# Cutting the second product of U's blocks into 24 and 232 columns, in 73 of 128 blocks

## The chip, the cores and the metric

The kernel runs on one core of a Trainium2 chip. The metric is the device time of one execution in microseconds (us). Before the change the median of 3 runs is 1714.33 us (1714.15 to 1714.38).

## The reference

The reference is two transformer blocks in a row on 256 tokens of 1024 features. The first has two kinds of attention and, at its end, a product-key layer of 128 x 128 = 16384 single-neuron experts. That layer is where the change is:

```python
def per_chunk(args):
    xc, ec, gc = args
    u = expert_u[ec]
    a = jnp.einsum('cd,chkd->chk', xc, u).astype(jnp.float32)
    w = (jax.nn.gelu(a) * gc).astype(xc.dtype)
    return jnp.einsum('chk,chkd->cd', w, expert_v[ec])
```

`expert_u` and `expert_v` are 16384 x 1024. The second block has self attention, cross attention and a gated feed-forward layer, the last with 5632 columns in its first product, in each of two layers.

## The kernel before

**The experts are not gathered.** The kernel multiplies all tokens by all of `expert_u`, 128 rows of experts at a time (a block of U: 1024 features by 128 experts, for 256 tokens), takes the gelu, weighs it by a dense table of gates that is zero for the experts not chosen, and multiplies by all of `expert_v`.

**Three products for one.** A float32 product is made of three. Each operand stands in SBUF as a high part and a rest (`wsplit[..., 0, ...]` and `wsplit[..., 1, ...]` for the weights, `HT[:, 0]` and `HT[:, 1]` for the normed input). `mm3` issues high x high, high x rest and rest x high into one PSUM area. A block of U has 8 tiles of 128 features (`k` from 0 to 7), so 24 products, each a weight load of 128x128 and a matmul that streams 256 columns of `HT`. "The second product" of the title is the tile k = 1, with its three matmuls.

**U has two stretches.** The first 16 blocks (`EARLY`, line 1463 on) write the ring of four PSUM banks and come before the table of gates can be begun. Six transposes follow (L1475), and then the other 112 blocks (`BULK`, `times_u` at L1478 on, loop at L1513). In front of 64 of these blocks, evenly from m = 2 on, `gate_products` issues four matmuls of 256 columns on one-hot matrices (`hot_a`, `hot_b`), which make the table of gates for four tokens. `hot_groups_at(m)` says whether a group stands before block m; there is never more than one.

**The order** is written out by hand, engine by engine. For U, ScalarE makes the high part of a block (L1967) when the block three places before has been multiplied, GpSimd makes the rest (L1657; VectorE for 14 of the early ones), and TensorE waits for that by `u_made(n)` and, from m = 2, for the gelu that empties its PSUM bank.

**A cut already stands elsewhere.** The first products of the feed-forward layers (`ffu`) go through `feature_tile`, which, for six of the first column tiles of each layer (`DIVIDED`), issues k = 1 by `mm3_divided`: the high x high matmul is cut into columns 0 to 23 and 24 to 255, so four matmuls and four weight loads in place of three. There the input `HT` also begins 16 float32 (64 bytes) further on in its tensor:

```python
DIVIDED = {"ffu": {(0, 1): 24, (1, 0): 24, (1, 1): 24, (2, 0): 24, (2, 1): 24, (3, 0): 24}}
HT_BEGINS = {"ffn0": 16, "ffn1": 16}
```

For U, `HT` is `HT_at("norm1")`, which begins at 0. In the built program HT lies at byte 22016 of a partition and wsplit at 38912, both multiples of 512; in the feed-forward layers the input therefore begins 64 bytes past such a multiple.

Of the kernel before, what the change touches and what calls it, by code (L numbers as in the profile page):

```python
# [15 lines left out]
S = 256  # L16
# [188 lines left out]
def block_stack(nc: bass.Bass, x, mem, weights, expert_u, expert_v, small, layer1, band, wide_gains, out):  # L205
    with ExitStack() as ctx:
# [20 lines left out]
        PS = [ctx.enter_context(nc.psum_tensor(f"bank{b}", [P, 512], F32))[:, :] for b in range(4)]  # L227
# [3 lines left out]
        def HT_at(name):  # L231

            at = HT_BEGINS.get(name, 0)
            return HT_room[:, at:at + 2 * KD * S].rearrange("p (b k s) -> p b k s", b=2, k=KD)

        HT = HT_at("norm1")
# [37 lines left out]
        c = Columns()  # L274
# [7 lines left out]
        c = Columns()  # L282
# [47 lines left out]
        c = Columns()  # L330
# [34 lines left out]
        def hot_block(g):  # L365

            return FIRST_HOT + g * HOT_SPAN // HOT_GROUPS

        def hot_groups_at(m):

            return [g for g in range(HOT_GROUPS) if hot_block(g) == m]
# [13 lines left out]
        def u_slot(n):  # L385

            return n % 3 + 1
# [9 lines left out]
        def u_made(n):  # L397

            if n in U_BY_VECTOR:
                return u_lo_v, n - U_BY_VECTOR.start + 1  # L400
            return u_lo, n + 1 - (len(U_BY_VECTOR) if n >= U_BY_VECTOR.stop else 0)
# [36 lines left out]
        c = Columns()  # L438
# [431 lines left out]
        def _(pe):  # L870
            state = {"frees": 0}

            def mm(out, lhsT, rhs, start, stop, **kw):

                ins = pe.matmul(out, lhsT, rhs, start=start, stop=stop, **kw)  # L875
                if state["frees"]:
                    ins.then_inc(w_freed, 1)
                    state["frees"] = 0
                return ins

            def mm3(out, left, right, start, stop, **kw):


                for n, (a, b) in enumerate(((0, 0), (0, 1), (1, 0))):
                    ins = mm(out, left(a), right(b), start and n == 0, stop and n == 2, **kw)
                return ins

            def mm3_divided(out, left, right, n):

                cols = out.shape[-1]  # L890
                for c in (slice(0, n), slice(n, cols)):
                    mm(out[:, c], left(0), right(0)[:, c], False, False, skip_group_check=True)
                mm(out, left(0), right(1), False, False, skip_group_check=True)
                return mm(out, left(1), right(0), False, False, skip_group_check=True)

            def weights_of(*name):

                u = UNIT[name]
                pe.wait_ge(*lo_made(u))
                state["frees"] = u not in (0, FIRST2)  # L900
                return lambda part: wsplit[:, u % NSPLIT, part, :]

            def tiles_of(w, **sizes):

                return lambda part: w(part).rearrange("p (k n) -> p k n", **sizes)

            def open_bank(name):

                q = GROUP[name]
                if q >= RING:  # L910
                    wait_freed(pe, GROUPS[q - RING][0])
                return PS[4 + q % RING]
# [279 lines left out]
            def first_branch(f):  # L1192

                b = open_bank(("up", f))
                w = tiles_of(weights_of("up", f), k=8)
                up_products(b, w, 0)
                return b, w
# [171 lines left out]
            for kv, at in enumerate((KC, VC)):  # L1369

                b = open_bank(("win2", kv))
# [11 lines left out]
            for kv in range(2):  # L1383

                b = open_bank(("hid", kv))
                for q in range(4):
                    w = tiles_of(weights_of("cmp", kv, q), k=4)
                    for kk in range(4):
                        k = 4 * q + kk
# [5 lines left out]
            for kv in range(2):  # L1395
                b = open_bank(("hidT", kv))
# [6 lines left out]
            for kv in range(2):  # L1403
                b = open_bank(("c2", kv))
# [13 lines left out]
            for f in range(KD):  # L1418
                if f < len(begun):
                    b, w = begun[f]  # L1420
                    state["frees"] = f > 0
                else:
                    b, w = first_branch(f)
# [14 lines left out]
            for m in range(8):  # L1438
# [11 lines left out]
                elif hp < 3:  # L1450
                    b = open_bank(("sc", m))
# [11 lines left out]
            for n in range(EARLY):  # L1463
                b = open_bank(("ua", n))
                pe.wait_ge(*u_made(n))
                w = tiles_of(lambda part: wsplit[:, u_slot(n), part, :], k=KD)
                for k in range(KD):
                    ins = mm3(b[:, 0:S], lambda a: w(a)[:, k, :], lambda c: HT[:, c, k, :], k == 0, k == KD - 1)
                ins.then_inc(bank_full, 1)
            pe.wait_ge(ex_done, 1)  # L1470
            for m in range(3):
                b = open_bank(("et", m))
# [5 lines left out]
            def times_u(m):  # L1478

                pe.wait_ge(*u_made(m + EARLY))  # L1480
                if m >= 2:
                    pe.wait_ge(a_gelu, m - 1)
                w = tiles_of(lambda part: wsplit[:, u_slot(m + EARLY), part, :], k=KD)
                for k in range(KD):
                    ins = mm3(PS[m % 2][:, 0:S], lambda a: w(a)[:, k, :], lambda c: HT[:, c, k, :], k == 0, k == KD - 1)
                ins.then_inc(a_full, 1)

# [25 lines left out]
            for m in range(BULK):  # L1513
                for g in hot_groups_at(m):
                    if g == 0:
                        for n in range(3):
                            wait_freed(pe, ("et", n))
                    gate_products(g)
                times_u(m)
# [30 lines left out]
            for m in range(5):  # L1550
                if m == 4:
                    values_of_memory(1, [0])
                b = open_bank(("qkt2", m))
# [11 lines left out]
            for i in range(DEPTH2):  # L1565
                if i:
# [4 lines left out]
                    for g in range(4):  # L1571
                        if g == 2:
                            mem_key(2, 1)
                        b = open_bank(("pm", g))
# [15 lines left out]
                    for g2 in range(2):  # L1590
                        w = weights_of("pool", g2)
# [74 lines left out]
        def _(act):  # L1666
# [110 lines left out]

            def attention(use, split_behind):
                _, _, Pb, Tb = USES[use]
                j0 = JOBS[use]  # L1780

# [356 lines left out]
        def _(dve):  # L2138
# [241 lines left out]

            def attention(use, last_queries):
                jobs, _, Pb, _ = USES[use]
                j0 = JOBS[use]

# [665 lines left out]
```

## Time and profile before

| | us |
|---|---|
| median of 3 runs | 1714.33 |
| the profiled execution | 1714.29 |
| its span in the trace | 1712.5 |
| TensorE busy | 1699.6 (99%) |
| VectorE, ScalarE, GpSimd busy | 1236.9, 919.6, 383.0 |
| all waits of TensorE that the profile lists, in the whole span | 6.2 |

The span is what the trace covers; 1.8 us of the execution lie around it. PE is TensorE's matmul, PEld its weight load. A row of the timeline joins neighbouring instructions of one kind: its first number is the start of the first, its second the time from there to the end of the last, so (second number - duration of one) / (count - 1) is the distance from start to start. A row joins matmuls of different widths when they have the same operands, and then names the width of the first. A matmul's duration (some 280 ns) is longer than the distance to the next, since matmuls overlap.

### The profile page before, as it was taken

Reading aid. Unit: us, or ns where it says so; the run is one execution under the profiler, and the core shown is the slowest. Engines: PE = TensorE matmul, PEld = TensorE weight load, DVE = VectorE, ACT = ScalarE, POOL = GpSimd, SP = SyncE. Lnnn points to the kernel's source line nnn. Section 1 sums busy time; section 2 is a strip of 40 time slices with the busy share of each in tenths; the row PEclk is TensorE's granted clock in tenths of the full one; section 3 lists DMA queues with packets and bytes.
Section 4 is the critical chain, followed back from the end, with each engine's and each line's share of the span. In section 5 each row is a group of like instructions: output and inputs, shape, how many; then the busy total and the mean of one; then the engine's idle time right before and its main releaser. Section 6 shows DMA issues by size and latency. Waiting matters only on the chain.

```text
span 1712.5 us, 31053 instructions
## 1 busy us (share of the span) xinstructions
PE 1699.6 (99%) x11336; PEld 1544.7 (90%) x11336; DVE 1236.9 (72%) x2436; ACT 919.6 (54%) x1449; POOL 383.0 (22%) x172
## 2 busy tenths in 40 slices
PE   9999999999999999999999999999999999999998
PEld 8897999899999999988888888877899988889997
DVE  6748749875555555488888887876789966769974
ACT  6568654554545555533333334576476645566653
POOL 1130077437777777500000000000000000000000
PEclk9999999999999999999999999999999999999999
DMA  8561665577777777777777797635545564445562
GB/s 307 197 238 36 193 197 171 199 218 211 206 210 207 212 205 211 226 246 242 238 241 243 266 328 235 231 131 172 198 167 196 197 204 149 164 147 184 190 208 72
DMA packets 120453, 346.54 MB, mean 202 GB/s; under 512 B 13328, under 2 KB 45200, under 8 KB 118928
## 3 DMA queue, kind: packets, MB, share of 16 engines
q1 hardware_dynamic: 118480, 336.70, 61.5%
q10 hardware_dynamic: 1856, 8.23, 1.3%
q8 instruction: 79, 1.29, 0.3%
q14 instruction: 38, 0.31, 0.1%
HBM read 321.03 MB, written 23.86 MB: 201 GB/s over the span
## 4 chain that ended last, share of the span: by engine, by line
PE 95%; ACT 2%; DVE 1%; issue 0%; DMA 0%; POOL 0%; ACTq 0%; DVEq 0%
PE banks L875 60%; PE bank L875 33%; PE bank L1279 1%; ACT wsplit L1680 0%; DVE wsplit L2147 0%; ACT probs L1832 0%; ACT H L1714 0%; PE banks L1279 0%; DMA X<-x 0%; PE bank L930 0%; ACT H L1720 0%; PE bank L1141 0%; PE banks L1092 0%; POOL wsplit L1657 0%; PE bank L942 0%
## 5 line engine op out<-in xcount | busy, mean ns | idle before, releaser
L875 PE MATMUL banks<-HT,wsplit 128*128 128x256 f32 (+1 forms) x3532 | 432.1, 284 | 1.3 <-POOL wsplit L1657 0.6
L875 PEld LDWEIGHTS banks<-HT,wsplit 128*128 128x128 f32 x3532 | 421.0, 189 | 10.3 <-issue 3.4
L1967 ACT ACTIVATE wsplit<-raw 128x1024 fp32r<-128x1024 f32 x252 | 266.4, 1058 | 212.2 <-PE banks L875 201.2
L875 PE MATMUL banks<-wsplit,wexp 128*128 128x512 f32 x1536 | 348.3, 389 | 0.0
L875 PEld LDWEIGHTS banks<-wsplit,wexp 128*128 128x128 f32 x1536 | 288.3, 188 | 59.7
L875 PE MATMUL bank<-HT,wsplit 128*128 128x256 f32 x2688 | 333.2, 283 | 0.0
L875 PEld LDWEIGHTS bank<-HT,wsplit 128*128 128x128 f32 x2688 | 327.2, 192 | 0.0
L1657 POOL TENSOR_TENSOR wsplit<-raw,wsplit 128x1024 fp32r<-128x1024 f32 x114 | 275.4, 2416 | 131.1 <-ACT wsplit L1967 131.1
L1680 ACT ACTIVATE wsplit<-raw 128x1024 fp32r<-128x1024 f32 x146 | 154.3, 1059 | 96.7 <-PE bank L875 48.1
L2147 DVE TENSOR_TENSOR wsplit<-raw,wsplit 128x1024 fp32r<-128x1024 f32 x124 | 151.6, 1235 | 67.3 <-ACT wsplit L1680 66.1
L2730 DVE TENSOR_TENSOR wsplit<-raw,wsplit 128x1024 fp32r<-128x1024 f32 x128 | 156.1, 1219 | 6.2 <-ACT wsplit L1967 6.2
L2751 DVE TENSOR_TENSOR gates<-banks,gates 128x512 f32<-128x512 f32 x64 | 44.3, 692 | 148.3 <-ACT gates L2031 148.3
L2147 DVE TENSOR_TENSOR wsplit<-raw1b,wsplit 128x1024 fp32r<-128x1024 f32 x101 | 121.4, 1220 | 41.1 <-ACT wsplit L1680 40.7
L1680 ACT ACTIVATE wsplit<-raw1b 128x1024 fp32r<-128x1024 f32 x102 | 107.6, 1059 | 73.8 <-PE bank L875 41.9
L875 PE MATMUL bank<-wsplit,ff 128*128 128x512 f32 x528 | 120.1, 389 | 0.0
L875 PEld LDWEIGHTS bank<-wsplit,ff 128*128 128x128 f32 x528 | 98.9, 188 | 20.6
L875 PE MATMUL banks<-wsplit,HT 128*128 128x512 f32 (+1 forms) x432 | 93.6, 378 | 0.0
L875 PEld LDWEIGHTS banks<-wsplit,HT 128*128 128x128 f32 x432 | 78.2, 188 | 14.9
L2870 DVE SCALAR_TENSOR_TENSOR cv<-banks,smalls,cv 128x255 f32<-128x255 f32 x176 | 76.9, 478 | 11.2 <-ACT cv L2119 8.4
L1629 POOL TENSOR_TENSOR wsplit<-raw,wsplit 128x1024 fp32r<-128x1024 f32 x20 | 48.0, 2402 | 164.9 <-ACT wsplit L1680 164.9
L2766 DVE CAST wexp<-act_e 128x256 fp32r<-128x256 f32 x126 | 37.1, 294 | 61.5 <-PE banks L875 61.4
L1661 POOL TENSOR_TENSOR wsplit<-raw1b,wsplit 128x1024 fp32r<-128x1024 f32 x1 | 2.4, 2409 | 349.5 <-DVE wsplit L2147 349.5
(333 smaller groups left out, 2022.6 us busy)
## 6 DMA issues: line engine op xcount, KB each, us to landing
raw<-weights SPq DMA_DIRECT2D x148, 512.0 KB, 4.0
raw<-expert_v SPq DMA_DIRECT2D x128, 512.0 KB, 3.6
raw<-expert_u SPq DMA_DIRECT2D x124, 512.0 KB, 3.9
raw1b<-weights SPq DMA_DIRECT2D x102, 512.0 KB, 4.2
raw1a<-weights SPq DMA_DIRECT2D x48, 512.0 KB, 4.5
HT<-acts_parked SPq DMA_DIRECT2D x124, 128.0 KB, 3.4
acts_parked<-act_e SPq DMA_DIRECT2D x62, 128.0 KB, 3.9
acts_parked<-ropeg SPq DMA_DIRECT2D x62, 128.0 KB, 3.8
```

Source lines behind the costliest of these rows:

```text
L875: ins = pe.matmul(out, lhsT, rhs, start=start, stop=stop, **kw)
L1279: ins = pe.transpose(turned_bank(use, j)[:, at:at + P], Pb[:, j % 4, t, kt * P:(kt + 1) * P], ident)
L1629: pool.tensor_tensor(wsplit[:, s % NSPLIT, 1, :], sb_raw(n0 + s), f32(wsplit[:, s % NSPLIT, 0, :]), ALU.subtract).then_inc(lo_made(n0 + s) ...
L1657: pool.tensor_tensor(wsplit[:, u_slot(n), 1, :], u_raw(n), f32(wsplit[:, u_slot(n), 0, :]), ALU.subtract).then_inc(u_lo, 1)
L1661: pool.tensor_tensor(wsplit[:, (FIRST2 + 1) % NSPLIT, 1, :], sb_raw(FIRST2 + 1), f32(wsplit[:, (FIRST2 + 1) % NSPLIT, 0, :]), ALU.subtract ...
L1680: act.activation(wsplit[:, u % NSPLIT, 0, :], sb_raw(u), ACT.Copy).then_inc(w_hi, 1)
L1967: act.activation(wsplit[:, s, 0, :], src, ACT.Copy).then_inc(e_hi, 1)
L2147: dve.tensor_tensor(wsplit[:, u % NSPLIT, 1, :], sb_raw(u), f32(wsplit[:, u % NSPLIT, 0, :]), ALU.subtract).then_inc(lo_made(u)[0], 1)
L2730: dve.tensor_tensor(wsplit[:, s, 1, :], raw0[:, s, :], f32(wsplit[:, s, 0, :]), ALU.subtract).then_inc(v_lo, 1)
L2751: dve.tensor_tensor(gates_of(g), hot_half(g, 0), gates_of(g), ALU.add).then_inc(hot_out, 1)
L2766: dve.tensor_copy(wexp[:, s % 2, 0, :], w).then_inc(a_hi, 1)
L2870: ins = dve.scalar_tensor_tensor(out=y, in0=u[:, v], scalar=w, in1=y, op0=ALU.mult, op1=ALU.add)
```

## The change

In the first six early blocks and in bulk blocks 0 to 5 and all in front of which one-hot products stand, tile k = 1 goes through `mm3_divided` with 24 columns. `mm3_divided` itself stands in the kernel before.

```diff
@@ early blocks
                 for k in range(KD):
+                    if n < 6 and k == 1:
+                        mm3_divided(b[:, 0:S], lambda a: w(a)[:, k, :], lambda c: HT[:, c, k, :], 24)
+                        continue
                     ins = mm3(b[:, 0:S], lambda a: w(a)[:, k, :], lambda c: HT[:, c, k, :], k == 0, k == KD - 1)
@@ times_u(m)
                 for k in range(KD):
+                    if (m < 6 or hot_groups_at(m)) and k == 1:
+                        mm3_divided(PS[m % 2][:, 0:S], lambda a: w(a)[:, k, :], lambda c: HT[:, c, k, :], 24)
+                        continue
                     ins = mm3(PS[m % 2][:, 0:S], lambda a: w(a)[:, k, :], lambda c: HT[:, c, k, :], k == 0, k == KD - 1)
```

That is 6 early blocks, and 64 + 3 = 67 bulk blocks (0, 1 and 4 have no one-hot products in front): 73 cuts, 73 more matmuls and weight loads. TensorE at the first early blocks, in the program before (`memN` is the turning of the memory that ends just before U):

```order
L978 MATMUL bank<-smalls,memN 128x128 x16
L875 MATMUL banks_7<-HT,wsplit 128x256 x24
L875 MATMUL banks_5<-HT,wsplit 128x256 x48
L875 MATMUL banks_7<-HT,wsplit 128x256 x48
```

and in the changed one:

```order
L978 MATMUL bank<-smalls,memN 128x128 x16
L875 MATMUL banks_7<-HT,wsplit 128x256 x3
L875 MATMUL banks_7<-HT,wsplit 128x24
L875 MATMUL banks_7<-HT,wsplit 128x232
L875 MATMUL banks_7<-HT,wsplit 128x256 x20
L875 MATMUL banks_5<-HT,wsplit 128x256 x3
L875 MATMUL banks_5<-HT,wsplit 128x24
```

Nothing is moved: one matmul of 256 columns has become two, at the fourth place of a block. In the bulk, TensorE around a group of one-hot products (`hot_a`), before:

```order
L875 MATMUL bank<-HT,wsplit 128x256 x48
L875 MATMUL banks_5<-wsplit,hot_a 128x256 x4
L875 MATMUL bank<-HT,wsplit 128x256 x48
L875 MATMUL banks_7<-wsplit,hot_a 128x256 x4
L875 MATMUL bank<-HT,wsplit 128x256 x24
```

and now:

```order
L875 MATMUL bank<-HT,wsplit 128x256 x44
L875 MATMUL banks_5<-wsplit,hot_a 128x256 x4
L875 MATMUL bank<-HT,wsplit 128x256 x3
L875 MATMUL bank<-HT,wsplit 128x24
L875 MATMUL bank<-HT,wsplit 128x232
L875 MATMUL bank<-HT,wsplit 128x256 x44
L875 MATMUL banks_7<-wsplit,hot_a 128x256 x4
```

After the cut, 20 products of its own block follow and, where no group stands before the next block, 24 of that. The other four engines have the same instructions in the same order.

## Rows read from the trace of the kernel before

**Rows 1.** The page, busy time and the chain that ended last.

```profile
PE 1699.6 (99%) x11336; PEld 1544.7 (90%) x11336; DVE 1236.9 (72%) x2436; ACT 919.6 (54%) x1449; POOL 383.0 (22%) x172
...
PE 95%; ACT 2%; DVE 1%; issue 0%; DMA 0%; POOL 0%; ACTq 0%; DVEq 0%
```

**Rows 2.** TensorE's waits from 321 to 721 us: total, times, longest.

```profile
PE banks L875 <- POOL wsplit L1657: 0.6, 1, 0.6
```

**Rows 3.** Stretches: U's bulk, V, feed-forward 0; busy time, clock, DMA.

```profile
core 0: us, PE busy (x) PEld busy (x) DVE busy (x) ACT busy (x) POOL busy (x), PEclk, DMA share, GB/s
367.70:721.10 353.40, 353.40 (x2947) 353.40 (x2946) 197.71 (x265) 180.98 (x291) 265.84 (x111) 1.00 0.73 209
721.10:1069.60 348.50, 348.37 (x1538) 288.24 (x1537) 279.83 (x510) 138.99 (x133) 2.41 (x1) 1.00 0.79 256
1254.30:1374.80 120.50, 120.50 (x1064) 120.50 (x1063) 110.74 (x191) 74.25 (x109) 0.00 (x0) 1.00 0.56 192
```

**Rows 4.** Timeline of TensorE in U's bulk: start, time, instructions.

```profile
500.32 0.64 PE L875 MATMUL banks<-wsplit,hot_a 128*128 128x256 f32 x4
500.80 5.92 PE L875 MATMUL bank<-HT,wsplit 128*128 128x256 f32 x48
506.56 0.64 PE L875 MATMUL banks<-wsplit,hot_a 128*128 128x256 f32 x4
```

**Rows 5.** Timeline of feed-forward 0 after its sixth cut.

```profile
1272.14 102.84 PE L875 MATMUL banks<-HT,wsplit 128*128 128x256 f32 x906
1374.82 0.39 PE L875 MATMUL bank<-wsplit,ff 128*128 128x512 f32 x1
```

**Rows 6.** Groups by shape: matmuls (PE) and weight loads (PEld), feed-forward 0, then U.

```profile
L875 PE MATMUL banks<-HT,wsplit 128*128 128x256 f32 x797 | 90.5, 276 | 0.0
...
L875 PE MATMUL bank<-HT,wsplit 128*128 128x256 f32 x2429 | 301.4, 283 | 0.0
...
L875 PEld LDWEIGHTS banks<-HT,wsplit 128*128 128x128 f32 x796 | 90.3, 188 | 0.0
...
L875 PEld LDWEIGHTS bank<-HT,wsplit 128*128 128x128 f32 x2428 | 295.8, 192 | 0.0
```

**Rows 7.** Timeline of feed-forward 0 up to its first cut and through it.

```profile
1254.34 3.23 PE L875 MATMUL banks<-HT,wsplit 128*128 128x256 f32 x26
...
1257.52 14.78 PE L875 MATMUL banks<-HT,wsplit 128*128 128x24 f32 x129
...
1257.55 1.16 PE L875 MATMUL banks<-HT,wsplit 128*128 128x232 f32 x8
...
1257.74 0.96 PE L875 MATMUL banks<-HT,wsplit 128*128 128x256 f32 x7
...
1257.86 0.84 PE L875 MATMUL banks<-HT,wsplit 128*128 128x256 f32 x6
...
1257.97 2.76 PE L875 MATMUL banks<-HT,wsplit 128*128 128x256 f32 x23
```

**Rows 8.** Timeline at the sixth cut of feed-forward 0.

```profile
1271.68 0.73 PE L875 MATMUL banks<-HT,wsplit 128*128 128x24 f32 x5
```

**Rows 9.** Timeline at the start of U's bulk, one start per row.

```profile
367.74 0.27 PE L1475 MATMUL banks<-smalls,pick 128*128 128x128 f32 x1
367.76 0.60 PE L875 MATMUL bank<-HT,wsplit 128*128 128x256 f32 x3
...
367.97 0.52 PE L875 MATMUL bank<-HT,wsplit 128*128 128x256 f32 x3
...
368.08 0.52 PE L875 MATMUL bank<-HT,wsplit 128*128 128x256 f32 x3
...
368.20 5.56 PE L875 MATMUL bank<-HT,wsplit 128*128 128x256 f32 x45
```

**Rows 10.** Timeline of the early blocks, after the wait of 0.6 us.

```profile
327.24 39.88 PE L875 MATMUL banks<-HT,wsplit 128*128 128x256 f32 x331
```

**Rows 11.** GpSimd's rests of U in 374 to 721 us; durations in ns.

```profile
L1657 POOL TENSOR_TENSOR wsplit<-raw,wsplit x109: 2396/2413/2417, 372.4 to 714.1; 128x1024 fp32r<-128x1024 f32 x109
its engine sat idle before it (us, times) until:
  ACT wsplit L1967: 82.5, 109
```

## The prediction

> **What bounds the kernel.** I read the page first: TensorE is busy for 99% of the span and holds 95% of the chain that ended last [rows 1]. Its waits come next: in all of U it waits once, for 0.6 us, before the bulk [rows 2]. The stretches say the same and give the clock: 353.4 us busy of 353.4 in the bulk at the full 2.4 GHz (granted clock 1.00) [rows 3]. So U lasts as long as the distance from one matmul's start to the next, times their number, and the question is what the cut does to that distance. A matmul more adds to the end; a shorter distance takes off it.
>
> **Two paces for the same instruction.** In the bulk, 48 products take 5.92 us with the last one's 0.28: 5.64 / 47 = 120.0 ns from start to start, and the one-hot groups keep it (500.32 to 500.80 is four times 120) [rows 4]. In the feed-forward layer, after its cuts, 906 products of the same shape run at (102.84 - 0.28) / 905 = 113.3 ns [rows 5]. The durations show the difference too: 276 against 283 ns for the matmul, 188 against 192 for the weight load [rows 6]. Before the first cut that stretch runs at neither: 1254.34 to 1257.52 for 27 products is 117.8 ns [rows 7]. So the feed-forward layer differs from U in two ways, the cut and the input that begins 64 bytes further on; without any cut it was already at 117.8 and not at 120.0, and the cut took it from there to 113.3. The trace has no cut over an input at 0 bytes. That is the unknown.
>
> **The price of a cut.** The four matmuls of a cut product start at 1257.52, 1257.55, 1257.74 and 1257.86, and the next one at 1257.97 [rows 7]: 0.34 us for the first three, then one ordinary distance of 0.11. From the first cut to the sixth there are 5 x 25 matmuls in 1271.68 - 1257.52 = 14.16 us, 113.3 ns each [rows 7, 8]: at the fast pace, a cut costs one whole distance, though its columns are the same 256.
>
> For U at 0 bytes the nearest rows are the start of the bulk [rows 9]. A narrow matmul (128 columns, 367.74) is followed 0.03 us later by one of 256, the next comes 0.21 us after that, then 0.11, then 0.12, and then 120 again. The same shape as the cut: 0.03, then a wide one that must wait for its own weights. With 232 columns in place of 256, 24 / 2.4 GHz = 10 ns come off, which gives the 0.19 of [rows 7]. For U I take 0.03 + 0.19 + 0.12 + 0.12, a shade less for the 0.11: 0.457 us for the four, against 3 x 0.120 = 0.360. One cut costs 0.097 us.
>
> A word on the weight load. The rows show 0.34 us for three matmuls that stream 512 columns (213 ns at 2.4 GHz), so the extra time is not streaming. The Trainium skill (TensorE: Matmul & The Clock Gate, "LDWEIGHTS (loading the stationary operand)") says that a load takes its columns over 1.2 GHz, so 107 ns here, and its section "Back-to-back issue gap" says that spacing is set by load and matmul together. By that, 73 cuts would cost 7.8 us at most, near my sum. The same section's formula for an isolated matmul (columns over 2.4 GHz and 2.5 ns) would make a cut nearly free, 0.2 us for all; the row of 0.19 us behind the 24 columns speaks against it, and I give that 1 in 100.
>
> **The sum.** 6 early and 67 bulk blocks are cut: 73 x 0.097 = 7.1 us, all on the path, since TensorE has no idle time to hide it in. The waits inside U don't grow: nothing is moved, and GpSimd, which makes the rests, is busy 2.41 us per block against 3.1 us of TensorE (347 us for 112 blocks) and waits 82.5 us for ScalarE, which waits for TensorE [rows 11]. A slower U gives it more room; a faster one (2.9 to 3.0 us per block) still leaves 0.5. V streams from its own loads after U and neither gains nor loses. Against the profiled execution: 1712.5 + 7.1 + 1.8 around the span = 1721.4 us. That execution's 1714.29 is the median of the runs within 0.04, so the forecast is **1721.4 us**. Bounds of one cut at an unchanged pace: 0.090 us if the four take 0.45 as in [rows 7], 0.101 if 0.461; so 6.6 to 7.4 us, 1720.9 to 1721.7. Allowing the first steps after a cut to be a few ns off on either side, this case's own range is 1720.4 to 1722.3.
>
> **Why the pace should stay at 120.** What a cut does is disturb the order in which matmul and weight load stand to each other. In U there are such disturbances already. At 367.76 the distances are 0.21, 0.11, 0.12 and then (5.56 - 0.28) / 44 = 120.0 ns [rows 9]. After the wait at 326 us the next 331 products run at (39.88 - 0.28) / 330 = 120.0 ns [rows 10]. At an input of 0 bytes every stretch that I followed came back to 120 within a few matmuls, also where one step of 113 or 114 ns stood in it; the 113.3 pace and the 117.8 pace are both seen only with the input at 64 bytes. A mechanism that fits: matmul and weight load walk through SBUF side by side (192 ns for the load in U, 188 in the feed-forward layer [rows 6]), and where both begin at the same offset they get in each other's way each time. The cut does not change the offset. That is an inference from one trace, and only the cut's own run can decide it.
>
> **Rivals.**
>
> *The cut sets the fast pace in U too* (28 in 100). For it: all 12 cuts in the two feed-forward layers are followed by 113.3, the first of them coming from another pace; 906 products then hold it across a wait per tile [rows 5, 7]. Against it: the offset, as above. Price: a cut block takes 25 x 113.3 = 2.833 us in place of 24 x 120 = 2.880, so 73 x 0.047 = 3.4 us gained; the other 10 early and 45 bulk blocks gain 24 x 6.7 ns = 0.160 us, 8.8 us; the 256 one-hot products gain 1.7 us if they hold the pace. In sum 13.9, and 10.9 if each one-hot group throws it back to 120 until the cut behind it (no 1.7, and 64 x 3 products at 120, 1.3 us): 1700.4 to 1703.4 us, 1702 in the middle. It decides from the point at which 15 products behind a cut run at 113.3, since 15 x 6.7 ns = 0.1 us pays for it.
>
> *The fast pace is set but lost at the end of the cut block* (8 in 100), by the waits that head each block. Then only the 73 x 0.047 = 3.4 us come: 1710.9 us. Against it: the feed-forward tiles have such waits and keep the pace.
>
> *An intermediate pace* (8 in 100), the 117.8 ns of [rows 7]. A cut block takes 0.457 + 21 x 0.1178 = 2.931 us, 0.051 more than now, an uncut one 2.827, 0.053 less: 73 x 0.051 - 55 x 0.053 = 0.8 us, less 0.5 for the one-hot products, 0.3 us more: 1714.6 us, no change. The nearly free cut (1 in 100) ends in the same place.
>
> *No lock* is the forecast, 54 in 100; 1 in 100 is left for what I don't see.
>
> **How the numbers follow.** A difference of 0.2% (3.4 us) is about what a measurement of this kernel can tell from none. Slower: the forecast and a little of the rest, 0.55. Faster: 28 and some two thirds of the 8 whose gain is right at the bound, 0.33. Within 0.2%: 0.12. The two large cases lie on both sides, so the range reaches from the middle of the fast one to the end of the slow one, 1702.0 to 1722.3, and leaves out about half of the fast case; the forecast's own range is 1720.4 to 1722.3.
>
> **What the changed profile would show.** The bulk's distance from start to start outside the cuts: 120.0 ns, matmuls of 283 ns and weight loads of 192, and U's bulk from 353.4 to 353.4 + 67 x 0.097 = 359.9 us. The four of a cut at 0.03, 0.19, 0.12, 0.12. V, and everything behind it, unchanged and 7.1 us later. It is wrong if matmuls of 276 ns stand in U: then the bulk lasts some 341 to 344 us, and the offset wasn't what kept U at 120. It is wrong in size if the steps after the 232 columns are not 0.12.

## The result, and the profile after

The changed kernel takes 1721.37 us (median of 6 runs, 1721.27 to 1721.51) against 1714.32 us for the kernel before beside it (6 runs, 1714.15 to 1714.51): ratio 1.0041, 95% interval 1.0031 to 1.0052. It is 7.05 us slower.

The page of the changed kernel, busy time and chain, in the form of [rows 1]:

```profile
PE 1707.6 (99%) x11409; PEld 1552.9 (90%) x11409; DVE 1236.9 (72%) x2436; ACT 919.8 (53%) x1449; POOL 382.3 (22%) x172
...
PE 96%; ACT 2%; DVE 1%; issue 0%; ACTq 0%; POOL 0%; DVEq 0%; POOLq 0%
```

73 matmuls and 73 weight loads more, TensorE busy 8 us longer, the other engines within 0.7 us of before. The stretches of U's bulk and of V, as in [rows 3]:

```profile
core 0: us, PE busy (x) PEld busy (x) DVE busy (x) ACT busy (x) POOL busy (x), PEclk, DMA share, GB/s
368.20:728.30 360.10, 360.10 (x3014) 360.10 (x3013) 197.60 (x265) 180.95 (x291) 265.21 (x111) 1.00 0.71 205
728.30:1076.80 348.50, 348.36 (x1538) 288.14 (x1537) 279.81 (x510) 138.99 (x133) 2.41 (x1) 1.00 0.79 256
```

The bulk grew by 6.7 us, which is 67 x 0.100; V is as long as before. The timeline of TensorE over the end of the bulk, as in [rows 4]:

```profile
709.87 0.64 PE L875 MATMUL banks<-wsplit,hot_a 128*128 128x256 f32 x4
710.35 6.02 PE L875 MATMUL bank<-HT,wsplit 128*128 128x256 f32 x49
716.21 0.64 PE L875 MATMUL banks<-wsplit,hot_a 128*128 128x256 f32 x4
716.69 11.78 PE L875 MATMUL bank<-HT,wsplit 128*128 128x256 f32 x97
728.31 2.00 PE L875 MATMUL banks<-wsplit,wexp 128*128 128x512 f32 x8
```

Two blocks, one of them cut, take 5.86 us from 710.35 to 716.21; in [rows 4] two uncut ones take 5.76. One cut at a time, here the start of each matmul from the narrow one on (each row is the first of an answer of its own, the window of each beginning one matmul later):

```profile
375.13 1.10 PE L875 MATMUL bank<-HT,wsplit 128*128 128x24 f32 x8
...
375.17 1.07 PE L875 MATMUL bank<-HT,wsplit 128*128 128x232 f32 x7
...
375.36 0.88 PE L875 MATMUL bank<-HT,wsplit 128*128 128x256 f32 x6
...
375.48 0.76 PE L875 MATMUL bank<-HT,wsplit 128*128 128x256 f32 x5
...
375.60 0.64 PE L875 MATMUL bank<-HT,wsplit 128*128 128x256 f32 x4
...
375.72 0.52 PE L875 MATMUL bank<-HT,wsplit 128*128 128x256 f32 x3
...
375.83 2.08 PE L875 MATMUL bank<-HT,wsplit 128*128 128x256 f32 x16
```

The steps are 0.03 (31 ns before the rows round it), 0.19, 0.12, 0.12, 0.12 and 0.11, and then (2.08 - 0.28) / 15 = 120.0 ns again. One step of 0.11 stands there, as it did after other disturbances, and the pace does not keep it. The groups by shape and the waits of the changed kernel, as in [rows 6] and [rows 2]:

```profile
L875 PE MATMUL bank<-HT,wsplit 128*128 128x256 f32 x2329 | 298.7, 283 | 0.0
...
L875 PEld LDWEIGHTS bank<-HT,wsplit 128*128 128x128 f32 x2445 | 296.5, 192 | 0.0
```

```profile
PE banks L875 <- ACT act_e L2012: 0.4, 1, 0.4
```

Still 283 and 192 ns. The one wait of the early blocks fell from 0.6 to 0.4 us: the first two cuts stand before it, and it still ended 6.6 us after U's start, so these two cost next to nothing.

### The profile page after: what moved, and what is told of

The parts are those of the page before. It is cut to its first block, busy times and chain, and to the rows that moved or that the text cites. A ratio compares the mean times of both kernels' runs of the same rounds, so it can differ in the third digit from the quotient of the medians.

```text
span 1719.6 us, 31199 instructions
## 1 busy us (share of the span) xinstructions
PE 1707.6 (99%) x11409; PEld 1552.9 (90%) x11409; DVE 1236.9 (72%) x2436; ACT 919.8 (53%) x1449; POOL 382.3 (22%) x172
## 4 chain that ended last, share of the span: by engine, by line
PE 96%; ACT 2%; DVE 1%; issue 0%; ACTq 0%; POOL 0%; DVEq 0%; POOLq 0%
PE banks L875 60%; PE bank L875 33%; PE bank L1279 1%; ACT wsplit L1686 0%; DVE wsplit L2153 0%; PE banks L1345 0%; ACT probs L1838 0%; ACT H L1720 0%; PE banks L1279 0%; PE bank L930 0%; ACT H L1726 0%; PE bank L1141 0%; PE banks L1092 0%; PE bank L942 0%; ACT HT L1744 0%
## 5 line engine op out<-in xcount | busy, mean ns | idle before, releaser
L875 PE MATMUL banks<-HT,wsplit 128*128 128x256 f32 (+2 forms) x3538 | 432.6, 284 | 1.1 <-ACT act_e L2012 0.4
L875 PE MATMUL bank<-HT,wsplit 128*128 128x256 f32 (+2 forms) x2755 | 339.9, 282 | 0.0
L875 PEld LDWEIGHTS bank<-HT,wsplit 128*128 128x128 f32 x2755 | 333.9, 192 | 0.0
```

## The experiments

All of them ask one question: is it the offset of the input that keeps U at 120 ns, and does the cut switch paces only where the offset allows it? The median in each row of the table is beside a baseline of its own series, 1714.26 to 1714.38 us. In the kernels that move the input of the second norm, the queries' 384 products read it too. For U three numbers are read from each trace's timeline: the early blocks (first product of U to the first of the six transposes), the bulk (its first product to V's first), and the pace.

| kernel | input of U at | cuts in U | early | bulk | median us |
|---|---|---|---|---|---|
| before | 0 | none | 47.0 | 353.4 | 1714.3 |
| changed | 0 | 73 | 47.4 | 360.1 | 1721.4 |
| off64_nocut | 64 bytes | none | 46.3 | 342.1 | 1701.1 |
| off64_cut | 64 | 73 | 45.3 | 344.0 | 1702.3 |
| off64_one_cut | 64 | 1 | 44.9 | 342.1 | 1701.0 |
| off128_nocut | 128 | none | 46.6 | 350.0 | 1710.3 |
| off192_nocut | 192 | none | 44.8 | 341.0 | 1698.4 |
| off256_nocut | 256 | none | 47.0 | 353.4 | 1714.2 |
| off448_nocut | 448 | none | 44.8 | 341.0 | 1698.6 |
| off512_nocut | 512 | none | 47.0 | 353.4 | 1714.2 |

### The offset alone, in U: off64_nocut

```diff
-HT_BEGINS = {"ffn0": 16, "ffn1": 16}
+HT_BEGINS = {"ffn0": 16, "ffn1": 16, "norm2": 16}
+        HU = HT_at("norm2")
...
-            norm_out("norm2", HT)
+            norm_out("norm2", HU)
```

HU stands in place of HT also in both loops of U and in the queries' products.

> The kernel before, with the input of the second norm (read by 384 products of the queries and by all 3072 products of U) beginning 64 bytes further on; no cut in U. Theory (the offset between the input and the weights decides which paces are possible): U leaves 120.0 ns for the 117.8 ns of the feed-forward layer before its first cut; about 3456 products x 2.2 ns = 7.6 us less, some 1706.7 us, weight loads of 188 ns. Rival 1 (what U lacks is the cut, the offset does nothing): 120.0 ns and 1714.3 us. Rival 2 (something in U holds the pace, GpSimd or the DMA traffic): also 1714.3 us, and then the next kernel too stays at 120.

Measured: 1701.11 us (1700.40 to 1701.62), ratio 0.9921 (0.9905 to 0.9938). The early blocks run at 117.8 ns, (39.81 - 0.28) / 335 = 118.0 with the slower first step behind the wait, as the theory said. Timeline of the early blocks after their wait, and of the bulk:

```profile
326.09 39.81 PE L876 MATMUL banks<-HT,wsplit 128*128 128x256 f32 x336 [0.75 <-POOL wsplit L1658]
```

```profile
375.73 5.82 PE L876 MATMUL bank<-HT,wsplit 128*128 128x256 f32 x48
381.38 0.65 PE L876 MATMUL banks<-wsplit,hot_a 128*128 128x256 f32 x4
381.87 5.61 PE L876 MATMUL bank<-HT,wsplit 128*128 128x256 f32 x48
387.31 0.64 PE L876 MATMUL banks<-wsplit,hot_a 128*128 128x256 f32 x4
387.79 2.99 PE L876 MATMUL bank<-HT,wsplit 128*128 128x256 f32 x24
```

My expectation of 1706.7 us failed in size, by 5.6 us, and nearly all of it lies in the bulk: 342.1 us, where 2688 products at 2.2 ns less each would have made 347.5. Its segments alternate: 5.54 / 47 = 117.9, then 5.33 / 47 = 113.4, then 2.71 / 23 = 117.8. At 64 bytes each group of one-hot products (both of its operands begin at a multiple of 512 bytes) throws the pace from the one to the other, in either direction, through all 65 segments. So nearly half of the bulk's products get the fast pace with no cut at all. Rivals 1 and 2 are excluded: the offset does nearly everything, with GpSimd and DMA as they were.

### Offset and cuts in U: off64_cut

The changed kernel with the same lines.

> The changed kernel with its 73 cuts, and the same 64 bytes. Theory (offset and cut together give the fast pace): 113.3 ns in U, 10.9 to 13.9 us below the kernel before plus up to 2.5 us from the queries, so 1698 to 1704 us. Rival 1 (U's stage forbids the fast pace): the cuts cost 7.1 us on top of whatever the offset alone gives, 1714 to 1721 us. If the one-hot products throw the pace back, the three products before each cut show 120 or 118 and the rest 113.3.

Measured: 1702.33 us (1701.92 to 1702.37), ratio 0.9929 (0.9912 to 0.9945), inside what was expected. At this offset the cut does switch:

```profile
380.53 0.64 PE L876 MATMUL banks<-wsplit,hot_a 128*128 128x256 f32 x4
381.01 5.73 PE L876 MATMUL bank<-HT,wsplit 128*128 128x256 f32 x49
386.58 0.64 PE L876 MATMUL banks<-wsplit,hot_a 128*128 128x256 f32 x4
```

The 49 matmuls with their cut take 5.57 us to the next group. Three products at about 119 ns, then the cut and everything behind it at 113.3, in every segment. The bulk is nevertheless 1.9 us longer than without cuts: every group now throws from 113.3 to the slower pace, and 67 cuts cost more than the further fast products win. The early blocks are 1.0 us shorter.

### The cuts without the offset, in the feed-forward layers: ffu_off0

```diff
-HT_BEGINS = {"ffn0": 16, "ffn1": 16}
+HT_BEGINS = {}
```

> The kernel before with its 12 feed-forward cuts kept, but the input of the feed-forward layers at 0 bytes, as in U. Theory (offset): the fast pace is gone there, 1056 products a layer at 120 and cuts at 0.457 us: 127.3 against 120.3 us per layer, +14.0 us, 1728.3 us. Rival (the cut alone sets the fast pace in this stage, U is different for another reason): 113.3 ns stays and the time is 1714.3 us.

Measured: 1727.86 us (1727.80 to 1727.94), ratio 1.0079 (1.0062 to 1.0095), 0.4 us from the theory. The timeline that answers to [rows 5]:

```profile
1272.76 109.00 PE L875 MATMUL banks<-HT,wsplit 128*128 128x256 f32 x907
```

(109.00 - 0.28) / 906 = 120.0 ns behind six cuts. The same stage, the same cuts, 64 bytes less: the fast pace is gone. This undoes exactly the part that U lacks.

### The offset without the cuts: ffu_nocut

```diff
-DIVIDED = {"ffu": {(0, 1): 24, ...}}
+DIVIDED = {}
```

> The kernel before with the input of the feed-forward layers at 64 bytes, without its 12 cuts. Theory (offset and cut are both needed for 113.3): both layers run at 117.8 ns throughout, 124.4 against 120.3 us per layer, +8.1 us, 1722.5 us. Rival (the offset alone reaches the fast pace sooner or later, as after the sixth cut): 12 x 0.113 us less for the cuts, 1713.0 us or a little more.

Measured: 1722.10 us (1722.06 to 1722.38), ratio 1.0045 (1.0029 to 1.0062), 0.4 us from the theory:

```profile
1254.51 124.42 PE L875 MATMUL banks<-HT,wsplit 128*128 128x256 f32 x1055
```

(124.42 - 0.28) / 1054 = 117.8 ns for a whole layer. At 64 bytes both paces hold by themselves.

### What a cut costs: cut_half

```diff
-mm3_divided(..., lambda c: HT[:, c, k, :], 24)
+mm3_divided(..., lambda c: HT[:, c, k, :], 128)
```

> The changed kernel, its 73 cuts at column 128 in place of 24 (input at 0 bytes as in it). Theory (a cut costs one more weight load, which lasts longer than 128 columns stream): two loads of about 110 ns for the two halves, 0.46 us for the four matmuls as before, 1721.4 us, within 1.5 us. Rival (the price comes from the narrow matmul that starts 30 ns before the wide one): clearly less, towards 1714.3 us.

Measured: 1721.44 us (1721.19 to 1721.48), ratio 1.0041 (1.0026 to 1.0056).

```profile
710.33 6.02 PE L875 MATMUL bank<-HT,wsplit 128*128 128x256 f32 x49
716.19 0.64 PE L875 MATMUL banks<-wsplit,hot_a 128*128 128x256 f32 x4
```

5.86 us again, as with 24 columns. The column of the cut doesn't matter at this offset: one more matmul with its weight load costs 0.100 us either way. That excludes the narrowness of the first part as the price. It fits the weight load as the price, but doesn't show it, since every cut adds a matmul and a load together.

### How few cuts: off64_one_cut

off64_nocut with `if n == 2 and k == 1: mm3_divided(...)` in the early blocks alone.

> The 64 bytes, and one cut alone, in the third early block (behind the wait for GpSimd). Theory (at 64 bytes both 117.8 and 113.3 are stable, a cut switches to 113.3, and a one-hot group switches from either to the other): the 14 early blocks behind the cut run at 113.3, 328 x 4.5 ns = 1.5 us less 0.1 for the cut, 1699.7 us; in the bulk the segments between one-hot groups alternate as without the cut. Rival (a single cut doesn't hold, six are needed as in the feed-forward layers): no gain over the 64 bytes alone, 1701.1 us.

```profile
326.02 37.99 PE L876 MATMUL banks<-HT,wsplit 128*128 128x232 f32 x333
```

From the 232 columns at 326.02 to the last start at 363.73 are 332 steps, the first 0.19, the others 113.3 ns: without a further cut the pace holds. The early blocks went from 46.3 to 44.9 us, the 1.4 that was forecast. The total missed its 1699.7: 1700.96 us, with runs from 1699.67 to 1701.55 (ratio 0.9922, 0.9909 to 0.9936), beside 1700.40 to 1701.62 without the cut on another chip. The profiled execution is the fastest of the five, and not only by the cut. The queries' products stand before any cut and are the same code in both kernels; here they are in this one and in off64_nocut:

```profile
225.80 12.63 PE L876 MATMUL banks<-HT,wsplit 128*128 128x256 f32 x110
```

```profile
225.72 13.23 PE L876 MATMUL banks<-HT,wsplit 128*128 128x256 f32 x111
```

(12.63 - 0.28) / 109 = 113.3 ns against (13.23 - 0.28) / 110 = 117.7. So at 64 bytes a stage can also enter either pace without a cut, behind its first waits, and two executions of the same instructions differ in it. Whether the single cut or the wait just before it set 113.3 in the early blocks isn't shown by one trace.

### Which offsets: 128, 192, 256, 448 and 512 bytes

The number behind "norm2" is 32, 48, 64, 112 and 128.

> The kernel before, with the input of the second norm 512 bytes further on, no cut in U. Theory (what counts is where input and weights begin within 512 bytes, and 64 bytes apart is what lets U run faster): 512 bytes are 0 again, 120.0 ns and 1714.3 us. Rival (any move of the input helps, by its distance from the weights or from what else lies there): like the 64 bytes, some 1701 us.

> The same with 256 bytes. If every offset but 0 keeps the two streams apart: 113 to 118 ns and 1694 to 1707 us. If the streams meet once in each product wherever they begin, and only 64 bytes puts the meeting where it costs little: 120.0 ns or more, 1714 us or more. I expect the first, with 0.6.

> The input of the second norm 128 bytes further on, no cut in U. 256 and 512 bytes left the pace at 120.0 ns where 64 took it to 113 to 118. Theory A (odd multiples of 64 bytes are fast, even ones slow): 120.0 ns, 1714.3 us. Theory B (a small distance is fast, by the few ns that one stream is ahead of the other): 113 to 118 ns, some 1701 us.

> The same with 192 bytes. Theory A (odd multiples of 64): fast, some 1701 us. Theory B (small distances alone): 120.0 ns and 1714.3 us.

> The same with 448 bytes, which is 64 bytes before the next multiple of 512. Theory A (odd): fast, some 1701 us. Theory B with a sign (the moving stream must be ahead, not behind): 120.0 ns and 1714.3 us; Theory B without one: fast.

Measured, in bytes: 512, 1714.24 us, ratio 1.0000 (0.9991 to 1.0009); 256, 1714.21 us, ratio 1.0000 (0.9990 to 1.0009); 128, 1710.30 us, 0.9977 (0.9967 to 0.9987); 192, 1698.44 us, 0.9908 (0.9890 to 0.9926); 448, 1698.60 us, 0.9909 (0.9891 to 0.9927).

256 bytes was a miss: I gave 0.6 to a fast pace, and U ran at (35.44 - 0.28) / 293 = 120.0:

```profile
327.77 35.44 PE L876 MATMUL banks<-HT,wsplit 128*128 128x256 f32 x294
```

The three odd multiples of 64 that were tried are fast without a cut. At 192 bytes the early blocks run at (37.45 - 0.28) / 328 = 113.3 ns, and the bulk alternates as at 64, but begins with the fast pace; at 448 it does the same. Most of the 2.7 us between 64 and 192 bytes comes from the pace with which each stretch began, so it isn't shown that 192 is the better offset.

```profile
325.73 37.45 PE L876 MATMUL banks<-HT,wsplit 128*128 128x256 f32 x329
```

```profile
373.46 3.01 PE L876 MATMUL bank<-HT,wsplit 128*128 128x256 f32 x24
```

The second row is of 128 bytes: 2.73 / 23 = 118.7 ns, steps of 115 to 122 ns mixed, so Theory A, which wanted 120.0 there, isn't the whole rule either. Theory B is excluded: 192 bytes is fast, which it denied without a sign, and 448 is, which it denied with one.

### The offset on the stationary side: off64_all

`HT_BEGINS` at 16 for the first and second norm, self attention, the cross attentions and the feed-forward layers.

> 64 bytes for the input of every norm that is kept in this tensor (first, second, self attention, both cross attentions, and the feed-forward layers as before), no cut in U: the version that may beat both. If the offset acts on all products of 256 columns: 384 more of the merge gates at 117.8, 0.8 us less than with the second norm alone. If it acts also where the input is the stationary side of 512 columns (432 products at 226.9 ns), up to 6.7 ns each, 2.9 us less. Sum: 1697.4 to 1700.3 us. Rival (512 columns are bound by their own streaming, and the cross attentions' mixed widths gain nothing): 1700.3 us or the 1701.1 us of the second norm alone.

Measured: 1702.48 us (1701.62 to 1703.11), ratio 0.9931 (0.9917 to 0.9944): not the 0.8 to 3.7 us of gain that I expected over the second norm alone, but 1.4 us slower than it by the medians, with intervals that overlap. U is as there (early 46.3, bulk 342.1 us). The group of 512 columns in which this tensor is the weights, before and in this kernel:

```profile
L875 PE MATMUL banks<-wsplit,HT 128*128 128x512 f32 x384 | 87.5, 389 | 0.0
```

```profile
L875 PE MATMUL banks<-wsplit,HT 128*128 128x512 f32 x384 | 90.0, 396 | 0.0
```

389 ns became 396, and 87.5 us became 90.0; from start to start it is 226.8 ns before and 233.3 now, in the mean. The offset acts on these too, but the other way: here 0 bytes is the better one.

## Why the prediction was right

**The bound.** TensorE held 99% of the span before and after, and every part of the difference lies on it.

**The price of a cut.** I took 0.457 us for the four matmuls and measured 0.463 (375.13 to 375.60); the three steps behind them are 3 ns shorter than three ordinary ones. So a cut costs 0.100 us and not 0.097, and the bulk says the same, 6.7 / 67. The term came from rows of another shape, the 128 columns at the start of the bulk [rows 9], less 10 ns for the narrower second part; the steps that these gave are those measured, to a few ns.

**The sum.** 67 x 0.100 = 6.7 us in the bulk as read. The 6 early cuts cost 0.6, of which the wait there gave 0.2 back. The step that had this wrong is "all on the path, since TensorE has no idle time to hide it in": the 0.6 us of [rows 2] was such time, and it hid the two cuts before it. The 0.1 by which U began later belongs to no step. 6.7 + 0.4 + 0.1 = 7.2 us, less under 0.1 in what follows: the span grew by 7.1. Two small errors of opposite sign, 0.2 each, met in my 7.1, so the agreement to the tenth is luck; the price of a cut and the pace are not.

**Why the pace stayed.** This was the step with the least under it, 54 in 100 against 28 for the fast pace. It came out as forecast, and the runs bear out its reason, the offset. ffu_off0, ffu_nocut and off64_cut show it in both places and both directions: an input at 0 bytes holds only 120.0, at 64 bytes 117.8 and 113.3 both hold, and a cut switches the slower to the faster. off64_nocut adds that the one-hot groups do that without a cut. The mechanism that I offered, two reads that get in each other's way where both begin at the same offset, is not shown, and as I put it it is wrong: at 256 bytes the two don't begin at the same offset, and U ran at 120.0 all the same. What the runs show is that the place within 512 bytes at which the streamed input begins decides which paces are possible; they don't show why. Only the input was ever moved, and the weights always began at a multiple of 512, so whether it is the distance between the two or the input's own address is open as well. The Trainium skill (TensorE: Matmul & The Clock Gate, "Step-by-step: what each phase is for") says that matmul and weight load have read ports of their own and that loading doesn't take read bandwidth from the running matmul. Here the measurement decides against drawing from it that addresses don't matter: 64 bytes on one side alone took off 13.3 us.

**The rivals.** The fast one, that the cut sets 113.3 in U too, needed the offset. With it added the cuts give 1702.3 us, next to the rival's 1702, but this is partly luck: 0.8 us of it comes from the queries, which the rival didn't price. In U alone off64_cut gains 1.7 us early and 9.4 in the bulk, 11.1 in all, and that is near the 10.9 that the rival gave for one-hot groups that throw the pace back, which is what the trace shows.

## What to carry to other kernels

When a stage is nothing but matmuls back to back, read the distance from start to start and compare it with the same shape elsewhere in the trace; here a difference of 5% between two stages pointed to 13 to 16 us. Before a trick is carried from one stage to another, list all in which the stages differ and undo these one at a time: here the cut was carried, and the 64 bytes that make it work stayed behind. The best version was neither kernel: the input of U at 192 bytes and no cut, 1698.4 us in 2 runs, 0.92% below the kernel before. And where a stage has two paces, one trace doesn't tell which it will take next time: compare several executions.

## What the runs showed of the hardware

A float32 product of 256 columns with a weight load each ran from start to start at 120.0 ns where the streamed input began 0, 256 or 512 bytes past a multiple of 512 and its weights at such a multiple, at 118.7 to 119.9 with 128, and at 113.3 or 117.8 with 64, 192 and 448. The last three have two paces that hold for hundreds of products, and four one-hot products in between were enough to go from one to the other; that it is the place of their operands that does it wasn't tested. At 64 bytes the same products of the queries ran at 113.3 ns in one execution and at 117.7 in another. One more matmul and weight load, by a cut at column 24 or 128, cost 0.100 us at 0 bytes. With 512 columns and the input as the weights, 64 bytes made the distance from start to start 6.5 ns longer.
